# Four gate tiles' borrowed rows copied by ScalarE and VectorE, and the decay moved from ScalarE to VectorE

## The reference, cut to what matters

```python
u = conv(u) + conv_b                                   # depthwise, width 4
ub = u.reshape(B, S, 16, 80)
r = sigmoid(einsum("bsnc,ncd->bsnd", ub, w_rg) + b_rg)
i = sigmoid(einsum("bsnc,ncd->bsnd", ub, w_ig) + b_ig)
log_a = -8.0 * r * softplus(-lru_lambda)
a = exp(log_a)                                         # the decay
b = sqrt(-expm1(2.0 * log_a)) * (i * u)
_, h = associative_scan(combine, (a, b), axis=1)       # h = a * h_before + b
lru_out = h * gelu(lru_y)
```

## Time and profile before

| what | value |
|---|---|
| median of 3 runs (lowest, highest) | 1619.98 us (1619.85, 1621.9) |
| the profiled execution, its own time | 1621.06 us |
| its span, first to last instruction | 1619.2 us |
| TensorE busy | 1603.6 us, 99% of the span, 7390 matmuls |
| GpSimd busy | 1234.4 us, 76% |
| VectorE busy | 905.0 us, 56% |
| ScalarE busy | 572.3 us, 35% |
| granted TensorE clock | 0.997 |

### The profile page before, as it was taken

One profiled execution on the slowest core, in us unless ns is written; L12 is line 12 of the kernel. 1 busy time (PEld: TensorE's weight loads), 2 busy tenths in 40 slices (PEclk: granted clock), 3 DMA queues, 4 the chain that ended last, 5 costly groups with the idle time before them and its releaser, 6 DMA issues.

```text
span 1619.2 us, 24286 instructions
## 1 busy us (share of the span) xinstructions
PE 1603.6 (99%) x7390; PEld 1327.0 (82%) x7390; DVE 905.0 (56%) x1158; ACT 572.3 (35%) x1078; POOL 1234.4 (76%) x1330
## 2 busy tenths in 40 slices
PE   9999999999999999999999999999999999999997
PEld 7888888888888888888888878888888888788887
DVE  6565646652165666676622579677865558405502
ACT  4787335532226885255422244100010013102100
POOL 5787866777777788777777777788887778877875
PEclk9999999999999999999999999999999999999999
DMA  5445432233344454522333583344422222733632
GB/s 165 131 120 131 132 91 80 74 101 93 97 144 128 121 133 114 166 77 74 92 97 95 150 286 107 97 118 117 119 75 75 65 65 69 245 93 114 222 107 87
DMA packets 121462, 188.86 MB, mean 117 GB/s; under 512 B 13668, under 2 KB 45796, under 8 KB 121380
## 3 DMA queue, kind: packets, MB, share of 16 engines
q1 hardware_dynamic: 97476, 144.03, 32.1%
q10 hardware_dynamic: 23904, 43.79, 8.2%
HBM read 162.73 MB, written 17.56 MB: 111 GB/s over the span
## 4 chain that ended last, share of the span: by engine, by line
PE 90%; DVE 4%; issue 2%; ACT 2%; ACTq 0%; DMA 0%; POOL 0%; DVEq 0%; SPq 0%; POOLq 0%
PE ps L872 14%; PE ps L871 14%; PE ps L870 14%; PE ps L1128 8%; PE ps L1127 8%; PE ps L1129 8%; PE ps L1225 4%; PE ps L1226 4%; PE ps L1227 4%; PE ps L950 1%; PE ps L946 1%; PE ps L947 1%; PE ps L1038 1%; DVE rows L2152 1%; DVE rows_r L2311 1%
## 5 line engine op out<-in xcount | busy, mean ns | idle before, releaser
L688 POOL TENSOR_TENSOR w_lo<-w_raw,w_hi 128x512 fp32r<-128x512 f32 (+2 forms) x374 | 448.3, 1199 | 31.2
L685 POOL TENSOR_SCALAR w_hi<-w_raw 128x512 fp32r<-128x512 f32 (+2 forms) x374 | 242.5, 648 | 194.4 <-PE ps L872 127.3
L872 PE MATMUL ps<-h_hi,w_lo 128*128 128x512 f32 x672 | 263.8, 393 | 0.0
L871 PE MATMUL ps<-h_lo,w_hi 128*128 128x512 f32 x672 | 263.6, 392 | 0.0
L870 PE MATMUL ps<-h_hi,w_hi 128*128 128x512 f32 x672 | 262.1, 390 | 0.7 <-DVE g_h L1950 0.6
L870 PEld LDWEIGHTS ps<-h_hi,w_hi 128*128 128x128 f32 x672 | 126.2, 188 | 28.9 <-DVE g_h L1950 1.5
L871 PEld LDWEIGHTS ps<-h_lo,w_hi 128*128 128x128 f32 x672 | 126.2, 188 | 27.5
L872 PEld LDWEIGHTS ps<-h_hi,w_lo 128*128 128x128 f32 x672 | 126.3, 188 | 26.1
L1127 PE MATMUL ps<-t,w_hi 128*128 128x512 f32 x352 | 138.2, 392 | 0.6 <-POOL w_lo L763 0.5
L1128 PE MATMUL ps<-t,w_hi 128*128 128x512 f32 x352 | 138.7, 394 | 0.0
L1129 PE MATMUL ps<-t,w_lo 128*128 128x512 f32 x352 | 136.6, 388 | 0.0
(11 more groups left out here) (389 smaller groups left out, 4105.7 us busy)
## 6 DMA issues: line engine op xcount, KB each, us to landing
w_raw<-w_f SPq DMA_DIRECT2D x68, 256.0 KB, 3.2
w_raw<-w_step SPq DMA_DIRECT2D x64, 256.0 KB, 2.8
w_raw<-w_b SPq DMA_DIRECT2D x64, 256.0 KB, 3.1
w_raw<-w_d SPq DMA_DIRECT2D x64, 256.0 KB, 2.7
w_raw<-w_a SPq DMA_DIRECT2D x96, 128.0 KB, 2.1
w_raw<-w_q SPq DMA_DIRECT2D x32, 256.0 KB, 3.1
w_raw<-w_o SPq DMA_DIRECT2D x32, 256.0 KB, 3.1
mix_hl<-uc_hl ACTq DMA_DIRECT2D x24, 256.0 KB, 4.7
```

Of the source, the lines that this page charges most:

```text
L685: nc.gpsimd.tensor_scalar(w_hi[:, s, w], w_raw[:, s, w], 1.0, 0.0, ALU.mult, ALU.add).then_inc(w_hi_made, 1)
L688: nc.gpsimd.tensor_tensor(w_lo[:, s, w], w_raw[:, s, w], rd(w_hi[:, s, w]), ALU.subtract).then_inc(w_lo_made, 1)
L871: mm(out, w_hi[:, s, w], x_lo, start=False, stop=False)
L872: last = mm(out, w_lo[:, s, w], x_hi, start=False, stop=(k == total - 1))
```

## The change

Tile 0 becomes a `NEAR` tile as well: its weights come as 128 own columns and 32 stacked rows by two loads, GpSimd splits them as for tiles 4, 5 and 9, and TensorE makes one matmul of 96 rows in the place of three. For all four `NEAR` tiles the 32 rows are no longer stacked by DMAs: ScalarE writes the two high copies (`near_rows_hi`, two activations on 32 rows), VectorE writes the low one (one subtraction on 32 rows, in `conv_lo`). TensorE waits for `near_hi_made` and `near_lo_made` where it waited for `mix_made`. The decay is a tensor_scalar of VectorE ahead of b, and ScalarE's `decay` is gone. `gate_fns` is cut in two: the high part of the new tile stands between the two Tanh and the Exp, and the DMAs of `mix` ahead of the Sqrt.

```diff
-NEAR = {4: (3, P - 32), 5: (6, 0), 9: (8, P - 32)}
-STACK = ((0, 0), (32, 1), (64, 0))
+NEAR = {0: (1, 0), 4: (3, P - 32), 5: (6, 0), 9: (8, P - 32)}
+NEAR_LIST = list(NEAR)
...
-                if j:
+                if j in MIXED:
                     pe.wait_ge(mix_made[j % 3], mix_count(h, j))
+                else:
+                    pe.wait_ge(near_hi_made, 2 * near_count(h, j))
+                    pe.wait_ge(near_lo_made, near_count(h, j))
...
+            def near_rows_hi(h, j, q):
+                for to, r in near_of(j):
+                    act.wait_ge(uc_hi_made, j + KR * h + 1)
+                    for row in (0, 64):
+                        fn(mix_hi[row:row + 32, to % 3, :], rd(uc_hi[r, q, :]), ACT.Copy)\
+                            .then_inc(near_hi_made, 1)
...
-                    elif to in NEAR and NEAR[to][0] == j:
-                        r = slice(NEAR[to][1], NEAR[to][1] + 32)
-                        for row, part in STACK:
-                            act.dma_start(rd(mix_hi[row:row + 32, to % 3, :]), rd(uc_hl[r, part, j % 4, :]))\
-                                .then_inc(mix_made[to % 3], 16)
...
-            def decay(h, j):
-
-                act.wait_ge(amp_made, j + KR * h + 1)
-                act.wait_ge(loss_made, j + KR * h + 1)
-                fn(g_a[:], g_r[:], ACT.Identity, bias=one_ap, scale=-1.0).then_inc(a_made, 1)
...
-                    gate_fns(h, j - 2, n + 2)
+                    gate_tanh(h, j - 2, n + 2)
                     conv_hi(h, j, j % 4)
+                    gate_exp(h, j - 2)
+                    mix(h, j)
                     gate_root(h, j - 2)
-                    mix(h, j)
-                    decay(h, j - 2)
+                    near_rows_hi(h, j, j % 4)
                     gelu(h, j, n + 6, j % 4)
...
+                for to, r in near_of(j):
+                    tt(mix_hi[32:64, to % 3, :], uc_of(q)[r, :], rd(uc_hi[r, q, :]), ALU.subtract)\
+                        .then_inc(near_lo_made, 1)
...
+                dve.wait_ge(loss_made, J + 1)
                 dve.wait_ge(amp_made, J + 1)
+                ts(g_a[:], g_r[:], -1.0, 1.0, ALU.mult, ALU.add).then_inc(a_made, 1)
```

More of the change, by code:

```diff
@@ L73, with near_count @@
 MIXED = (1, 2, 3, 6, 7, 8)
-NEAR = {4: (3, P - 32), 5: (6, 0), 9: (8, P - 32)}
-STACK = ((0, 0), (32, 1), (64, 0))
+NEAR = {0: (1, 0), 4: (3, P - 32), 5: (6, 0), 9: (8, P - 32)}
+NEAR_LIST = list(NEAR)
 STACKED = 96
 def mix_count(h, j):
-    same = range(j % 3, KR, 3)
-    dmas = [2 if i in MIXED else len(STACK) if i in NEAR else 0 for i in same]
-    return 16 * (h * sum(dmas) + sum(dmas[:j // 3 + 1]))
+    same = [i for i in MIXED if i % 3 == j % 3]
+    return 32 * (h * len(same) + same.index(j) + 1)
+def near_count(h, j):
+    return len(NEAR) * h + NEAR_LIST.index(j) + 1
 GATED = {"step": 0, "tail": 8}
@@ L399, in build @@
             sem("a_made"), sem("gelu_made"), sem("lru_hi_made"))
+        near_hi_made, near_lo_made = sem("near_hi_made"), sem("near_lo_made")
         iu_made, loss_made, amp_made, b_made, scanned, h_kept, lru_made, lru_lo_made = (
@@ L505, in a21_there, with near_of @@
             return (up_one_loaded[1], 16) if t == 1 else (up_loaded[1], 16 * single_loads(t))
+        def near_of(j):
+            return [(to, slice(r, r + 32)) for to, (of, r) in NEAR.items() if of == j]
         block = ctx.enter_context(nc.Block())
@@ L536, in load_gates @@
                             .then_inc(w_loaded[s], 16)
-                    elif i not in NEAR:
-                        sp_eng.dma_start(w_raw[:, s, 0:2 * P], dram[g, :, off:off + 2 * P])\
-                            .then_inc(w_loaded[s], 16)
                     else:
-                        own = off + P
+                        own = off + (P if i else 0)
                         near, r = off if NEAR[i][0] < i else own + P, NEAR[i][1]
@@ L545, in load_gates @@
                                          .rearrange("(o r) c -> o r c", o=1)
-                                         .broadcast_to([len(STACK), 32, P])).then_inc(mix_loaded[s], 16)
+                                         .broadcast_to([STACKED // 32, 32, P])).then_inc(mix_loaded[s], 16)
                         sp_eng.dma_start(w_raw[:, s, 0:P], dram[g, :, own:own + P])\
@@ L711, in split_gates @@
                     pool.wait_ge(w_loaded[s], (n // RING + b // RING + 1) * 16)
-                    if size < 4 and i:
+                    if size < 4:
                         used[s] += 2 if i in MIXED else 1
@@ L920, in gates @@
                     if j not in NEAR:
-                        near_hi, near_lo = ((mix_hi[:, j % 3, :], mix_lo[:, j % 3, :]) if j else
-                                            (uc_hi[:, 1, :], uc_lo[:, 1, :]))
+                        near_hi, near_lo = mix_hi[:, j % 3, :], mix_lo[:, j % 3, :]
                         mm(out, w_hi[:, s, near], near_hi, start=False, stop=False)
@@ L1406, in gate_fns, with gate_exp @@
                     .then_inc(i_made, 1)
+            def gate_exp(h, j):
+                J = j + KR * h
                 act.wait_ge(r_made, J + 1)
@@ L1446, in recurrent @@
                     conv_hi(h, j, j)
+                    near_rows_hi(h, j, j)
                     mix(h, j)
@@ L1501, in kvq @@
                         keys(0, NCH * h)
-                    gate_fns(h, 8 + p, n + 4 * p + 2)
+                    gate_tanh(h, 8 + p, n + 4 * p + 2)
+                    gate_exp(h, 8 + p)
                     gate_root(h, 8 + p)
-                    decay(h, 8 + p)
                 lru_out_hi(h, 9)
```

3 lines of the change are left out of this document (1 added, 2 removed).

## The result

The changed kernel takes 1633.38 us in the median (1632.28 to 1636.06, 4 runs), before in the same job 1620.5 (1619.85 to 1621.9): a ratio of 1.008, interval [1.0066, 1.0094]. It is 12.9 us slower, outside the range. The profiled execution took 1632.28 us with a span of 1630.3, 11.1 more than before.

The account below looks back on a forecast made before the run. TensorE's matmuls were taken as the bound, with tail waits on tile 9's scan. Matmuls -1.83, earlier DMAs -0.63 and tail +4.3 summed to +1.9 us, a median of 1621.8 us, range 1618.3 to 1625.3.

Parts of the forecast that it names:

- the decay's cover: In the ten steps, VectorE's decay lies beside 12 to 14 us of matmuls; only the tail has no such cover.
- the early high part: High part behind the two Tanh, so `mix` DMAs come some 2 us earlier: gain 0.63 us, bounds 0 and 0.63.
- The rival: Tile 0 waits for copies, or Exp behind the high part delays a later step; +3.9 us, 1623.8; chance 0.04.
- late copies: Same rival's other case: tile 0's gates wait for the copied rows, needing more than 1.5 us to spare.
- Matmuls, -1.83: Tile 0's gates on TensorE: eight matmuls fewer at 0.228 us each, -1.83 us.
- Copies, nothing: ScalarE and VectorE copies replacing DMAs stand beside TensorE's work; cost nothing, 1.5 us to spare at tile 0.
- Earlier DMAs, -0.63: Pauses ahead of the gates of tiles 6 and 7 (0.24, 0.15, 0.24 us) all go: -0.63 us.
- Tail, +4.3: Decay on VectorE, with GpSimd's conflicts, ends tile 9's scan 2.16 us later per half, delaying second q projections: 4.3 us.
- the sign "none" at the second q projection: TensorE showing no pauses at the second q projection, where the forecast expected about 2.4 and 2.9 us.
- the faster rival: In the tail `amp` no longer meets a `w_lo`, pauses of 0.28 and 0.72 vanish: -3.5 us, 1616.5; chance 0.06.

Follow-up runs that it names:

- e4: Kernel before with ScalarE's new order alone (early high part, DMAs ahead of the Sqrt; rows by DMA, decay on ScalarE): 1630.39 us, ratio 1.0066.
- e8: Changed kernel with GpSimd's low part of the wide blocks cut from 512 columns to 16, that computation left out: 1625.1 us, ratio 1.0031.
- e10: Kernel before with the new order alone, and GpSimd's low part of the wide blocks cut from 512 columns to 16: 1622.43 us, ratio 1.0016.
- e13: Changed kernel with VectorE's convolution ahead of the product and ScalarE's `lru_hi` behind the third Tanh: 1629.58 us, ratio 1.0059.
- e15: Changed kernel with convolution ahead of the product, `lru_hi` behind the third Tanh, and the decay of tiles 8 and 9 on ScalarE: 1623.96 us, ratio 1.0022.
- e7: Changed kernel with ScalarE's old order and the decay on ScalarE; copied rows and tile 0's matmul stay: 1619.4 us, ratio 0.999 against before.
- e5: Kernel before with the decay on VectorE and nothing else: 1626.88 us, ratio 1.0049.
- e16: Changed kernel with the decay of tiles 8 and 9 alone on ScalarE again: 1628.54 us, ratio 1.0053.
- e6: Changed kernel with ScalarE's whole old order put back, decay on VectorE and copied rows kept: 1630.14 us, ratio 1.005.

## Why the prediction was wrong

**The step that failed** is the decay's cover, "In the ten steps it lies beside 12 to 14 us of matmuls, and ScalarE no longer waits in `decay`" (there are eight steps a half), together with the early high part, priced between 0 and -0.63 us. Matmuls beside a chain hide it only if the chain's whole round is shorter than a step, and the round was never added up. The early high part put the convolution into the round, the decay put itself there, and with GpSimd's holds it became up to 15.3 us against 13.7. Shown: e4 (the order alone, +10.4, in a ring over the Gelu), e8 and e10 (without the holds 8.5 and 9.0 us come back), e13 (rounds fall to 13.4 to 14.0 once convolution and `lru_hi` leave it). Not shown is what holds the +3.7 us that are left in e15 with the ring cut and the tail's decay back.

**The rival** that named this, an Exp behind the high part delaying a later step, had a chance of 0.04 and a price of 1 us a half. Its other sign, late copies, came too, though not at tile 0: 1.24 us ahead of tile 5's gates.

**Matmuls, -1.83:** right, 7390 - 7382 = 8. **Copies, nothing:** right by e7, not in the late ring of the changed kernel (tile 5, above). Tile 0's copies and its low rows ended at 42.63 and 42.74, TensorE came at 44.30 and did not wait.

**Earlier DMAs, -0.63:** two of the three pauses are gone; tile 7's in the first half grew, by starts from 0.06 to 0.44 us.

**Tail, +4.3:** mechanism right, size a little off where it can be seen alone. e5's pauses grew by 1.87 (0.28 to 2.15) and 1.78 us (0.72 to 2.50), 3.65 in the place of 4.3; the decay takes 0.426 us alone, 0.41 was taken. By the Trainium skill's "SBUF — State Buffer", section "Who interferes with whom", the loser of the shared port stands for the winner's whole instruction; the decays up to 1.339 us agree. In the changed kernel the pause came earlier, at v, a wait for the scan of tile 8 that I had not looked for, and it was fed by lag of the steps as well as by the tail's own decay (e16: 4.6 us of it). So the sign "none" at the second q projection, which stood for the faster rival, came in a slower kernel. The half clock behind a pause, 1.5 to 1.7 us each time, stood in no term.

## What to carry to other kernels

Where two engines hand a tile back and forth, follow the hand-overs until they close, add up the round with the durations that occur under contention, and compare it with the step of the bounding engine before calling anything hidden. Moving an instruction earlier is free only if its input is there: look at what it waits for at the new place and at everything behind it on its engine. A lag need not show where it arises: look for the waits at which the bounding engine next needs the ring's result.

## What was not expected of the hardware

After the pauses of 3.5 us in v the granted clock was 0.50 and came back to 1.00 within some 4 us; after e5's pause of 2.50 us it was 0.50 from 646 to 648 us too. After e5's pause of 2.15 us, in the first half, and e15's at v it stayed at 1.00 in every window of 2 us behind them. The length of a pause alone does not tell which will come: behind e6's first one of 2.20 us at the second q projection the clock was 0.50 from 184 to 186 us, behind e8's two of 2.48 and 2.50 it stayed at 1.00.
